# Moving a four-byte tensor ahead of the weight copies in a decoder-layer kernel

## The reference

```python
c_act = jax.nn.silu(c)
mod = (c_act @ w_mod[l] + b_mod[l])[:, None, :]          # 2048 x 12288
sh1, sc1, g1, sh2, sc2, g2 = jnp.split(mod, 6, axis=-1)
h = rms_norm(x, norm1_g[l]) * (1.0 + sc1) + sh1
z = h @ w_in[l]                                          # 2048 x D_IN, then split by heads
mixed = jnp.concatenate([o_fox, o_nsa, o_conv], axis=-1) # forgetting attention, sparse attention, convolution
x = x + g1 * (mixed @ w_out[l])                          # 2048 x 2048
h = rms_norm(x, norm2_g[l]) * (1.0 + sc2) + sh2
x = x + g2 * (jnp.square(jax.nn.relu(h @ w_mlp1[l])) @ w_mlp2[l])   # 2048 x 8192 and 8192 x 2048
return rms_norm(x, final_g)
```

## The kernel before

| tensor | first byte, before | remainder by 64 |
|---|---|---|
| `raw0` to `raw3` (8192 bytes each) | 16512 | 0 |
| `w_hi0` to `w_hi3` (4096 each) | 49280 | 0 |
| `w_lo0` to `w_lo3` (4096 each) | 65664 | 0 |
| `mod_raw0`, `mod_raw1` (8192 each; later also `t_hi`, `t_lo`, `acc_hi`, `acc_lo`) | 82048 | 0 |
| `acc0`, `acc1` (8192 each; later also `s_hi`, `s_lo` of number 1 and 2) | 98432 | 0 |
| `ident` to `b_col` (ten small tensors) | 114816 | 0 |
| `seen` (4 bytes) | 118784 | 0 |
| `arena` (holds `u_hi`, `u_lo`, `x2`, `y`, `fox_hi`, `conv_hi`, `late_raw`, ...) | 122272 | 32 |
| `hold` (holds `act`, `nsa_hi`, `end_hi`, `end_lo`, ...) | 192416 | 32 |
| `early3` (later also `s_hi0`, `s_lo0`, `ones_r`) | 225184 | 32 |

## Time and profile before

### The profile page before, as it was taken

How to read it: one execution, slowest core, us unless ns; L and a number is a source line. 1 busy time by engine, 2 the same in 40 slices (tenths; PEclk the granted TensorE clock), 3 DMA queues, 4 the chain that set the end, 5 groups by cost and what they waited for, 6 DMA issues and landing times.

```text
span 1172.2 us, 17842 instructions
## 1 busy us (share of the span) xinstructions
PE 1134.7 (97%) x7087; PEld 1005.2 (86%) x7087; DVE 983.7 (84%) x1182; ACT 641.5 (55%) x936; POOL 23.6 (2%) x40
## 2 busy tenths in 40 slices
PE   4999999999999999999999999999999999999996
PEld 4899989999887778999788888888888888888885
DVE  5998989988997988997887788987778987878774
ACT  6655458877775546544454445554455544445452
POOL 1000000100000000010000000000000000000000
PEclk6999999999999999999999999999999999999999
DMA  9999998878966897985657675657674667666451
GB/s 372 420 420 420 421 409 310 255 205 281 358 227 249 301 304 292 401 351 183 210 186 266 240 282 180 215 187 277 238 270 176 218 202 263 251 231 262 152 180 72
DMA packets 48322, 314.65 MB, mean 268 GB/s; under 512 B 6572, under 2 KB 8440, under 8 KB 11768
## 3 DMA queue, kind: packets, MB, share of 16 engines
q1 hardware_dynamic: 44592, 305.72, 70.1%
q0 software_dynamic: 1760, 5.26, 2.4%
q10 hardware_dynamic: 1896, 2.64, 0.8%
HBM read 305.20 MB, written 4.21 MB: 264 GB/s over the span
## 4 chain that ended last, share of the span: by engine, by line
PE 76%; DVE 11%; DMA 5%; ACT 4%; issue 3%; SPq 0%; ACTq 0%; DVEq 0%
PE quad L1285 15%; PE quad L1299 10%; PE quad L1300 10%; PE quad L1301 10%; PE quad L1287 8%; PE quad L1275 5%; PE quad L1276 5%; PE quad L1277 5%; DMA first_raw<-in_w_mod 3%; DVE w_lo L1850 3%; PE quad L1346 2%; PE quad L1345 2%; PE quad L1347 2%; DVE mod_raw L1857 2%; DMA mod_raw<-in_w_mod 2%
## 5 line engine op out<-in xcount | busy, mean ns | idle before, releaser
L893 ACT ACTIVATE w_hi<-raw 128x1024 fp32r<-128x1024 f32 (+1 forms) x342 | 355.4, 1044 | 304.9 <-PE quad L1301 115.9
L1850 DVE TENSOR_TENSOR w_lo<-raw,w_hi 128x1024 fp32r<-128x1024 f32 (+1 forms) x342 | 408.3, 1204 | 112.4 <-ACT w_hi L893 110.4
L1285 PE MATMUL quad<-act,w_hi 128*128 128x512 f32 x768 | 266.4, 390 | 0.0
L1275 PE MATMUL quad<-act,w_hi 128*128 128x256 f32 x760 | 215.2, 283 | 6.0 <-DVE w_lo L1850 3.9
L1287 PE MATMUL quad<-act,w_lo 128*128 128x256 f32 x768 | 216.6, 282 | 0.0
L1276 PE MATMUL quad<-act,w_hi 128*128 128x256 f32 x760 | 213.1, 280 | 0.0
L1277 PE MATMUL quad<-act,w_lo 128*128 128x256 f32 x760 | 213.1, 280 | 0.0
L1285 PEld LDWEIGHTS quad<-act,w_hi 128*128 128x128 f32 x768 | 144.2, 188 | 30.2
L1275 PEld LDWEIGHTS quad<-act,w_hi 128*128 128x128 f32 x760 | 144.1, 190 | 8.7 <-issue 4.6
L1299 PE MATMUL quad<-w_hi,u_hi 128*128 128x512 f32 x376 | 148.8, 396 | 0.6 <-DVE u_lo L2307 0.6
L1301 PE MATMUL quad<-w_hi,u_lo 128*128 128x512 f32 x376 | 148.7, 396 | 0.0
(11 more groups left out here) (371 smaller groups left out, 1715.6 us busy)
## 6 DMA issues: line engine op xcount, KB each, us to landing
raw<-in_w_main SPq DMA_DIRECT2D x184, 1024.0 KB, 5.0
mod_raw<-in_w_mod SPq DMA_DIRECT2D x67, 1024.0 KB, 7.2
first_raw<-in_w_mod SPq DMA_DIRECT2D x14, 1024.0 KB, 15.3
late_raw<-in_w_mod SPq DMA_DIRECT2D x10, 1024.0 KB, 7.9
acc<-in_w_mod SPq DMA_DIRECT2D x4, 1024.0 KB, 12.5
conv_b<-conv_q POOLq DMA_DIRECT2D x8, 512.0 KB, 5.2
x_a<-in_x SPq DMA_DIRECT2D x2, 1024.0 KB, 7.2
x_scratch<-x SPq DMA_DIRECT2D x1, 2048.0 KB, 11.7
```

The costliest lines, as they stand in the source:

```text
L893: A(dst[:, 0:2 * width], block_half(raw, j, width), ACT.Copy).then_inc(hi_done, 1)
L1275: mm(out, hi, act_hi[:, k, :], start=begin and m % 2 == 0, stop=False, skip_group_check=True)
L1285: mm(out, w_hi[j % 4][:, cols], act_both[:, k, :, :].rearrange("p h t -> p (h t)"), start=begin, stop=False, skip_group_check=True)
L1850: TTn(lo[:, 0:2 * width], block_half(raw, j, width), hi[:, 0:2 * width].bitcast(f32), ALU.subtract)\
```

## The change

The allocation of `seen` moves from behind `b_col` to between `raw` and `w_hi`. It takes 32 bytes, so all that is allocated between the two places begins 32 bytes further: `w_hi`, `w_lo`, `mod_raw`, `acc` and the ten small tensors from `ident` to `b_col`, with all that is laid over `mod_raw` and `acc`. `raw` stays, and so does everything from `c_col` on, `arena`, `hold` and `early3` among it.

```diff
         raw = [sb(f"raw{i}", [P, 4 * GW]) for i in range(4)]
+        seen = sb("seen", [P, 1])
         w_hi = [sb(f"w_hi{i}", [P, 2 * GW], f32r) for i in range(4)]
         w_lo = [sb(f"w_lo{i}", [P, 2 * GW], f32r) for i in range(4)]
         mod_raw = [sb(f"mod_raw{i}", [P, D]) for i in range(2)]
...
         m_sum = sb("m_sum", [P, 4 * KT])
         m_col = sb("m_col", [P, 4 * KT])
         b_col = sb("b_col", [P, 4 * KT])
-        seen = sb("seen", [P, 1])
         c_col = sb("c_col", [P, KT])
```

## The result

The kernel after takes 1175.57 us, median of 20 runs, against 1173.7 us for the kernel before beside it: ratio 1.0019 with a 95% interval of 1.0012 to 1.0025, so it is 1.4 to 2.9 us slower. One of the 20 executions, at 5427.77 us, is left out of the ratio. The forecast was 1163.5 us. The place of the operands does set what a matmul costs, and `token_rows` got the nanoseconds that it was to get. But the matmuls that were costed at nothing changed too, and nearly all of them for the worse.

What follows compares the result with a forecast made beforehand. PE was taken to bound the kernel from 562 to 1164 us. Span 1172.2 - 7.0 - 2.6 is 1162.6, plus 0.9 around it 1163.5 us; own range 1158 to 1168, 8 times in 10 1150 to 1175 us.

Steps and rivals of the forecast that it cites:

- What bounds the kernel: Whole span: DVE and a weight load before 112 us, PE about three fifths to 562, then all PE to 1164.
- PE, the moving operand: L1299 to L1301 on `w` buffers: remainder 32 saves 6.6 ns per matmul, 7.0 us after 562 us and 2.6 before.
- PE, the stationary operand and 256 columns: `merged_rows`, `feature_rows`, `split_half`: taken at 0, with bounds of 13.0 us faster and 12.9 us slower.
- DVE, ACT and DMA at 0: Subtraction, copies and loads on shifted operands: no cost, with 1.2 us as the upper bound for slower loads.
- The 2.6 us in 112 to 562 us: L1299 to L1301 in that stretch, 92.7 us of chain by 2.83%: 2.6 us gained, bounds 0 and 2.6.
- Rival 1: Low memory region, not remainder, makes 512-column moving operands slow; nothing changes, 1173.1 us; chance 0.19.
- Rival 2: Stationary operand gains too: 256-column matmuls at 113.3 ns, 13.0 us more off, 1150.5 us; chance 0.22.
- Rival 3: Stationary weights at the activations' remainder slow `merged_rows` and `feature_rows`, no `token_rows` gain: 12.9 us slower, 1186 us; chance 0.13.

Runs made afterwards that it cites:

- e5: Kernel before with weight buffers 4608 bytes apart, copies for `token_rows` 32 bytes into them, all others at their start: 1166.92 us, ratio 0.9937.
- d000: Kernel before with `arena` 224 bytes up, `hold` and `early3` 288 down, weights unmoved: 1175.14 us, executed once.
- e6: As e5, with `feature_rows` weights in a third place of the buffers, at distance 64 by 256: 1164.07 us, ratio 0.9911 against the kernel before.
- e4: Kernel before with padded weight buffers 4160 bytes apart, half j of every weight group 8 x j bytes (0 to 56) into its buffer: 1178.9 us, one execution.

## Why the prediction was wrong

- **What bounds the kernel**: right. With no instruction moved the time followed PE's nanoseconds, and no other engine became the bound; DVE has 75.83 us in 897:983 us where it had 73.53.
- **PE, the moving operand**: the size was right, 390 ns and 5.5 ns less between starts where 6.6 were forecast, -9.1 us over 1656 matmuls against -9.6. The cause was wrong, so the size came out by luck: the 32 bytes brought `w` to the remainder of `end` and also to its distance. The pair of rows it was read from, `w` and `end`, differ not only in the remainder of the moving operand but also in its distance to the stationary one: `end` stands at 0 by 256 from `u`, `w` at 32. In every run here `end` keeps that distance, whatever its remainder, and its matmuls stand 226.7 to 228.3 ns apart. "It isn't the stationary operand either, which is the same" was the slip: it is the same, but the distance to it is not.
- **PE, the stationary operand and 256 columns**: this is the step that failed. It was taken at 0 with bounds of -13.0 and +12.9 us; measured are +6.1 (L1285), -1.0 (L1287), +5.5 (L1275 to L1277) and +0.8 (L1345 to L1347), +11.4 us. The row that it was taken from, L1285 at 390 ns with its stationary operand at 0, was read as "no penalty for its stationary operand at 0", and showed a good distance, 224, which the change then took away.
- **DVE, ACT and DMA at 0**: right, to 3 ns in an instruction of DVE or ACT. Loads into `mod_raw` land after 7.1 us and not 7.2, into `late_raw`, which didn't move, after 8.4 and not 7.9.
- **The 2.6 us in 112 to 562 us**: not separated. With `token_rows` alone gaining (e5) the runs show 5.8 to 8.9 us, 5.7 of them from the down projection on in its trace, which leaves 0 to 3 for what lies before.
- **Rival 1**, the region: out. The weights stayed in the low region and took 390 ns (d000: unmoved).
- **Rival 2**, 256 columns at 113.3 ns: not here, but it was seen later at another distance, in the up projection of e6. Its price took the starts of before too high: by the table (116.75, 118.3 and 118.4 ns) it would have been 11.8 us and not 13.0.
- **Rival 3**, slower: L1285 and `feature_rows` did get slower with their stationary weights at the remainder of `act` (399 and 283 ns), and its 12.9 us were near the 11.4 measured; but L1287, priced at +2.3, got quicker by 1.0, and the remainder isn't the cause. It was tied to rival 1, no gain in `token_rows`; the argument against it, that in the `end` rows both operands are at 32 and quick, had no force, since the same distance is good there and bad here. The combination that came, gain and loss at once, had no case: -9.1 and +11.4 make +2.3, and the range stopped 0.6 us below the time.

## What to carry to other kernels

When a row is explained by an address, list the addresses of both operands, and their difference, before naming a cause: two forms that differ in one remainder differ in the distance too. A change that moves one operand of many forms is to be priced for each form with the sign open, and gains in one are not to be tied to the absence of losses in another. Where PE is the chain, the place of a buffer can be chosen for each kind of matmul apart: 32 to 96 bytes of padding, in buffers kept a multiple of 256 bytes apart, were worth 0.5 to 1% here. With buffers 4160 bytes apart the gain was gone.

## What the runs showed of the hardware

PE's distance between starts depends on the address distance between stationary and moving operand, and it came back whenever the distance changed by 256 bytes: 227.8 to 234.6 ns for one sequence of 512 columns, 228.3 to 236.2 for another, and 113.3 to 120.0 for 256 columns, all at a granted clock of 1.00, the 2.4 GHz level. The distance doesn't fix it alone: at 0 L1285 has a pattern of 236.2 ns in the mean and one of 230 (the kernel after and e4), and at 64 the 256 columns stand 113.3 or 117.8 ns apart within one trace (e6). On the page of the profile PEld, the load of the next stationary operand, overlaps PE; that the two reads meet is a natural reading of a distance that counts, but no run here took the load away, so it isn't shown. The Trainium skill, in "SBUF — State Buffer", section "A bandwidth-pool intuition that's wrong (but worth ruling out)", names a second independent read port of PE for weight loads. If that is taken to mean that the two reads never hinder each other, the distance shouldn't matter. Here it does: the run with both moved by 32 bytes kept all lengths, and the one with the activations alone moved didn't (L1285 396 ns against 390).

In L1345 to L1347 of the kernel after, with all at distance 0, each pair of `t` and `s` buffers has 120.0 ns between starts, where before had 116.3 to 121.5 at 32 and 118.3 to 119.9 at 0. The pairs that stood at 0 already changed as well, which again fits that the matmuls around one count.
